# A two-block kernel on one core: which accumulator pair a stream begins on, and where its residuals stand

## What is computed

```python
hx = _rmsnorm(x, norm_g[l]) * (1.0 + scale) + shift        # scale, shift, gate: silu(c) @ w_mod[l]
hc = _rmsnorm(ctx, norm_g[l]) * (1.0 + scale_c) + shift_c
q, k, v, g_att, u_pool, g_pool, a_conv, b_conv, g_conv = split(hx @ w_in[l])
...
y = concat([y_att * silu(g_att), y_pool * silu(g_pool), y_conv * silu(g_conv)])
x = x + gate * (y @ w_out)                                  # and for ctx in layer 0
```

## Time and profile before

| | us |
|---|---|
| median of 3 runs (2693.75 to 2694.1) | 2694.1 |
| the profiled execution | 2695.04 |
| its span | 2693.1 |
| TensorE busy in it | 2604.9 (97%) |
| VectorE busy | 1701.3 (63%) |
| ScalarE busy | 1259.4 (47%) |
| mean granted TensorE clock | 0.993 of full |

### The profile page before, as it was taken

The page is one execution under the profiler, slowest core; times in us unless marked ns, Lnnn a source line. Parts: engine busy times, 40 slices in busy tenths (PEclk is TensorE's granted clock), DMA queues, the critical chain, the costliest instruction groups (busy, mean ns, idle before and its releaser), DMA issues.

```text
span 2693.1 us, 34021 instructions
## 1 busy us (share of the span) xinstructions
PE 2604.9 (97%) x12453; PEld 2064.8 (77%) x12453; DVE 1701.3 (63%) x2483; ACT 1259.4 (47%) x1734; POOL 101.0 (4%) x147
## 2 busy tenths in 40 slices
PE   7999999999999999798999999999999999999997
PEld 5888888888877776565788787678878886788876
DVE  5565755656644444354678856388985664688855
ACT  4544544545533333343356553345554443345553
POOL 0000000000000000000200000020000000200000
PEclk9999999999999999899999999999999999999999
DMA  7555555555568888868854567864446758844454
GB/s 239 172 183 169 179 174 172 165 180 172 171 235 289 291 275 293 279 242 324 277 168 157 168 239 261 314 213 139 161 150 219 244 185 317 279 141 156 136 182 152
DMA packets 350381, 569.62 MB, mean 212 GB/s; under 512 B 18096, under 2 KB 202832, under 8 KB 346272
## 3 DMA queue, kind: packets, MB, share of 16 engines
q1 hardware_dynamic: 343248, 531.48, 58.0%
q0 software_dynamic: 6992, 36.18, 3.9%
HBM read 559.17 MB, written 8.42 MB: 211 GB/s over the span
## 4 chain that ended last, share of the span: by engine, by line
PE 81%; DVE 8%; issue 4%; DMA 4%; ACT 2%; SPq 1%; DVEq 1%; POOL 0%; ACTq 0%
PE acc L451 24%; PE acc L453 23%; PE acc L452 23%; PE aux L971 3%; DMA raw<-in_w_mod 2%; DVE w_lo L439 2%; PE aux L1173 1%; DVE cacc L2332 1%; DVE sm L2264 1%; PE aux L1306 1%; ACT w_hi L431 1%; PE aux L1146 1%; DMA xr_s<-x_mid 1%; DMA xr_s<-c_mid 1%; PE aux L878 1%
## 5 line engine op out<-in xcount | busy, mean ns | idle before, releaser
L439 DVE TENSOR_TENSOR w_lo<-raw,w_hi 128x1024 fp32r<-128x1024 f32 x808 | 989.1, 1229 | 763.6 <-ACT w_hi L431 761.8
L431 ACT ACTIVATE w_hi<-raw 128x1024 fp32r<-128x1024 f32 x808 | 846.7, 1058 | 928.4 <-PE acc L453 867.3
L451 PE MATMUL acc<-w_hi,h_hi 128*128 128x512 f32 x2240 | 894.7, 399 | 11.6 <-DVE w_lo L439 4.5
L453 PE MATMUL acc<-w_hi,h_lo 128*128 128x512 f32 x2240 | 873.6, 390 | 0.0
L452 PE MATMUL acc<-w_lo,h_hi 128*128 128x512 f32 x2240 | 873.4, 390 | 0.0
L451 PEld LDWEIGHTS acc<-w_hi,h_hi 128*128 128x128 f32 x2240 | 421.0, 188 | 145.0 <-issue 53.1
L453 PEld LDWEIGHTS acc<-w_hi,h_lo 128*128 128x128 f32 x2240 | 420.7, 188 | 90.3
L452 PEld LDWEIGHTS acc<-w_lo,h_hi 128*128 128x128 f32 x2240 | 421.4, 188 | 81.9
L451 PE MATMUL acc<-w_hi,u_hi 128*128 128x512 f32 x800 | 320.7, 401 | 4.4 <-ACT cT L1765 2.3
L452 PE MATMUL acc<-w_lo,u_hi 128*128 128x512 f32 x800 | 312.1, 390 | 0.0
L453 PE MATMUL acc<-w_hi,u_lo 128*128 128x512 f32 x800 | 312.0, 390 | 0.0
(11 more groups left out here) (348 smaller groups left out, 1892.1 us busy)
## 6 DMA issues: line engine op xcount, KB each, us to landing
raw<-in_w_in SPq DMA_DIRECT2D x632, 512.0 KB, 4.4
raw<-in_w_mod SPq DMA_DIRECT2D x192, 512.0 KB, 6.1
raw<-in_w_out SPq DMA_DIRECT2D x96, 512.0 KB, 5.0
raw<-in_w_rnn_out SPq DMA_DIRECT2D x32, 512.0 KB, 5.1
raw<-in_w_o SPq DMA_DIRECT2D x32, 512.0 KB, 6.1
raw<-in_w_attn_out SPq DMA_DIRECT2D x16, 512.0 KB, 5.8
xr_s<-x_mid POOLq DMA_DIRECT2D x4, 1024.0 KB, 12.6
xo<-x_mid POOLq DMA_DIRECT2D x4, 1024.0 KB, 8.0
```

The lines of the kernel that those rows point to most:

```text
L431: act.activation(w_hi[:, n % NSPLIT], raw[:, slot, (n % 2) * SK:(n % 2) * SK + SK], ACT.Copy).then_inc(hi_ready, 1)
L439: dve.tensor_tensor(w_lo[:, n % NSPLIT], raw[:, slot, (n % 2) * SK:(n % 2) * SK + SK], w_hi[:, n % NSPLIT].bitcast(F32), ALU.subtract).the ...
L451: pe.matmul(acc[pair][m][:, :], a_hi[:, k0 + k, tok], w_hi[:, s, k], start=b, stop=False)
L453: last = pe.matmul(acc[pair][m][:, :], a_lo[:, k0 + k, tok], w_hi[:, s, k], start=False, stop=e)
```

## The change

Two things, both in the hand-written order. First, `FLIP` gives each stream a bit; stream x0 has 1. All its accumulator uses are turned over, on each engine: the first four parts, the head parts, the transposes that borrow a pair, the last input part and the output parts. `pair_free` for x0 and c1 now waits for residual 2's reads in part 0 and for residual 3's in part 1. Second, residuals 0 to 2 of each tail stand at `out_end(c) + 4` (25, 27 and 35), and residual 3 at granule 4 of the following stream. PE's waits for parts 2 and 3 stay as they were.

```diff
+        FLIP = (0, 1, 0, 0)
...
-                    pe.wait_ge(*ST[s - 1].at("res", 2 * NT * (NCH - 1) + NT) if c == 0 else ST[s - 1].at("res", 2 * NT * (NCH - 1)))
+                    pe.wait_ge(*ST[s - 1].at("res", 2 * NT * (NCH - 2 + c) + NT))
...
-                        products(pe, q, n, c % 2, 2 * g, a_hi, a_lo, g == 0, g == 7)
+                        products(pe, q, n, (c + flip) % 2, 2 * g, a_hi, a_lo, g == 0, g == 7)
...
-                    products(pe, q, n, (c + 1) % 2, 2 * j, b_hi, b_lo, j == 0, j == 7)
+                    products(pe, q, n, (c + 1 + flip) % 2, 2 * j, b_hi, b_lo, j == 0, j == 7)
...
+                pair = [acc[(i + FLIP[s]) % 2] for i in range(2)]
...
-                    if n == 1:
+                    if n == 4:
                         last_stage_end()
...
-                    if s == 1 and n == 1:
+                    if s == 1 and n == 4:
                         last_stage_end()
...
-                        dve.tensor_tensor(ytmp[:, m], acc[(c + 1) % 2][m][:, :], gbc[:, cs], ALU.mult).then_inc(S["res"], 1)
+                        dve.tensor_tensor(ytmp[:, m], pair[(c + 1) % 2][m][:, :], gbc[:, cs], ALU.mult).then_inc(S["res"], 1)
...
                     for c in range(NCH - 1):
-                        if n == out_end(c) + 2:
+                        if n == out_end(c) + 4:
                             residual(c)
```

More of the change, by code:

```diff
@@ L1278, in stream @@
                             for j in range(4):
-                                last = pe.transpose(acc[1][m][:, j * P:(j + 1) * P], cacc[:, j, m * P:(m + 1) * P], ident[:, :])
+                                last = pe.transpose(acc[1 - flip][m][:, j * P:(j + 1) * P], cacc[:, j, m * P:(m + 1) * P], ident[:, :])
                         last.then_inc(S["cb_ps"], 1)
@@ L1288, in stream @@
                             for m in range(NT):
-                                last = pe.transpose(acc[1][j // 2][:, (2 * (j % 2) + m) * P:(2 * (j % 2) + m + 1) * P],
+                                last = pe.transpose(acc[1 - flip][j // 2][:, (2 * (j % 2) + m) * P:(2 * (j % 2) + m + 1) * P],
                                                     tcy[:, m, j * P:(j + 1) * P], ident[:, :])
@@ L1690, in stream @@
                         done(3)
-                        act.activation(stg[:, 1], acc[0][1][:, :], ACT.Copy).then_inc(S["ev_act"], 1)
+                        act.activation(stg[:, 1], pair[0][1][:, :], ACT.Copy).then_inc(S["ev_act"], 1)
                     if n == 31:
@@ L1703, in iteration @@
                                 done(4)
[L1704 to L1705 removed]
+                                act.activation(stg2[:, 0], pair[1][0][:, :], ACT.Sigmoid)
+                                act.activation(stg2[:, 1], pair[1][1][:, :], ACT.Sigmoid).then_inc(S["ev_act"], 1)
                             if n == 8:
@@ L1731, in iteration @@
                             act.wait_ge(*S.at("qkT_ps", 2 * p))
-                            act.activation(qk2[:, 1], acc[0][1][:, :], ACT.Copy).then_inc(S["ev_act"], 1)
+                            act.activation(qk2[:, 1], pair[0][1][:, :], ACT.Copy).then_inc(S["ev_act"], 1)
                         if n == 15:
@@ L2362, in stream @@
                             dve.wait_ge(*ST[2].at("kT_ps", 2))
-                        dve.tensor_copy(stg[:, 0], acc[0][0][:, :]).then_inc(S["ev_dve"], 1)
+                        dve.tensor_copy(stg[:, 0], pair[0][0][:, :]).then_inc(S["ev_dve"], 1)
                     if n == 19:
@@ L2427, in iteration @@
                             dve.wait_ge(*S.at("qkT_ps", 2 * p))
-                            dve.tensor_copy(qk2[:, 0], acc[0][0][:, :]).then_inc(S["ev_dve"], 1)
+                            dve.tensor_copy(qk2[:, 0], pair[0][0][:, :]).then_inc(S["ev_dve"], 1)
                             if not rotary:
@@ L2449, in conv_norm @@
                         for m in range(NT):
-                            step.link(dve.bn_stats(bns[:, m], acc[1][m][:, :]))
+                            step.link(dve.bn_stats(bns[:, m], pair[1][m][:, :]))
                         step.wait(dve)
@@ L2460, in conv_norm @@
                         for m in range(NT):
-                            step.link(dve.tensor_scalar(tcy[:, m], acc[1][m][:, :], sm[:, 48 + 2 * m:49 + 2 * m], sm[:, 46 + m:47 + m],
+                            step.link(dve.tensor_scalar(tcy[:, m], pair[1][m][:, :], sm[:, 48 + 2 * m:49 + 2 * m], sm[:, 46 + m:47 + m],
                                                         ALU.subtract, ALU.mult))
```

33 lines of the change are left out of this document (17 added, 16 removed).

## The result

The changed kernel is slower: 2705.3 us (median of 7 runs, 2703.2 to 2708.5) against 2694.3 for the kernel before (7 runs, 2693.8 to 2700.5), a ratio of 1.0032 with a 95% interval of [1.0022, 1.0041]. A second measurement gave 2704.3 against 2696.7, 1.0028 [1.0018, 1.0039]. The forecast was 2701.0, in a range of 2694.5 to 2705.5.

What follows compares the result with a forecast made beforehand. TensorE, busy 97% of the span, was taken as the bound, so only its pauses count. Tails +5.9, clock +4.2, stream starts -3.4, `w_mod` granule +0.9, x1's tail -0.7: +6.9 us, median 2701.0, range 2694.5 to 2705.5.

Steps and rivals of the forecast that it cites:

- Part 1, the tails: Tails of c0 and x0: residual 0 behind the sums delays TensorE before granule 24; net +2.95 and +2.93, together +5.9 us.
- Part 2, the clock: Behind each new 3.9 us tail pause the clock likely falls to half, 8 in 10 each; +4.2 us for both.
- rival A: Tail pauses come but the clock holds in both or one: 2696.8 us, or 2698.9 with one fall; chance 0.22.
- Part 3, the stream starts: Starts of x0 and c1: TensorE's wait for residual 3 to free `acc[0]` goes at both; -3.4 us.
- Part 3, the third `w_mod` granule: Start of x0: the later `c_mid` write meets this granule's load; +0.9 us, bounds -1 to +3.
- Rival C: Start of x0: `c_mid` write costs its upper bound and the fourth `w_mod` granule is late too; 2704 us, chance 0.11.
- Part 4: Tail of x1, without normalization: `lo(24)` and `lo(25)` run first and residual 0 frees the pair in time; -0.7 us.
- Rival B: Early tails: the `xr_s` load lands early enough that residual 0 is not held; -5.4 us, 2688.7, chance 0.11.
- Rival D: Stream starts gain nothing, as a late split granule or last normalization replaces the wait; +3.4 us, 2704.4, chance 0.06.

Runs made afterwards that it cites:

- second profile: Profile of the changed kernel, unedited, measured once more beside the kernel before: 2704.3 us, ratio 1.0028 [1.0018, 1.0039].

## Why the prediction was right, and where its sizes were off

**Part 1, the tails.** Right. TensorE was due at 1606.76 and 2084.54 (the last matmul before the pause, plus 0.227 us) and went on at 1610.89 and 2088.75: 4.13 and 4.21 us late, against 4.08 and 4.03 forecast. The pauses before 26 are gone, and so is that of the last tail; residuals 1 and 2 cost nothing.

**Part 2, the clock.** Right in kind and a little too dear: a fall behind each pause, 1.7 us each in the first profile against 2.1 forecast. In the second profile TensorE resumed at 1606.58 with the clock already at half, and it was back at 1612.8: 6.2 us of work at half, 3.1 lost, by this stretch:

```profile
1612.00:1613.00 1.00, 1.00 (x5) 0.76 (x4) 0.97 (x3) 0.84 (x1) 0.00 (x0) 0.60 0.92 256
```

The net of each tail, pause and clock, is +4.6 and +4.8 by the time from the stage's first matmul to the normalization's transposes (51.37 and 51.46 us, against 46.73 and 46.71); forecast +5.0 each. The chances did not fit each other: 8 in 10 for each fall leaves 0.36 for rival A if the two are independent, not 0.22.

**Part 3, the stream starts.** The waits went as said. The step at each start is 0.23 us where it was 1.81, so -1.6; what S3 leaves after its tail is -1.9; forecast -1.7 each. c1's ScalarE waits 1.91 us for its rows, forecast 2, and no one waits for it.

**Part 3, the third `w_mod` granule, is the term that was mis-sized**: +0.9 taken, bounds -1 to +3. It waits 3.31 instead of 1.01 us, and the clock fell behind it, 1.7 us more: about +4. In the second profile no fall, but 3.51 + 0.80 us of waits: +3.3.

Two things were off. The first is the landing. Counted from the last matmul of c0 (1650.61 before, 1659.81 after), TensorE asked for the granule at 19.10 instead of 20.78, so 1.7 us earlier, just as forecast. It got it at 22.41 instead of 21.79, so 0.6 later, where +0.9 means about 0.8 earlier. The issue by SyncE, forecast 0.6 earlier, came at 10.91 instead of 10.95, and its two transfers took 2.79 us to go out instead of the 1.06 of the earlier trace rows:

```profile
1670.72 2.79 SPq L377 DMA_DIRECT2D raw<-in_w_mod  x2
```

The second is the clock, which the forecast priced in the tails only. Rival C named the place and took the upper bound; its number, 2704, is nearer.

**Part 4.** -1.1 against -0.7.

The sum over the touched stages by these measures is 4.6 + 4.8 - 1.6 - 1.9 + 3.8 - 1.1 = +8.6 (the table's +8.7, rounded otherwise), against +6.9 forecast; the 3.8 is what S1 leaves after its tail and start. With +4.6 ahead of S1, -1.0 in S2 and 0 in S4, from the clock's falls there, this is the +12.1 between the two profiled spans. The medians differ by 11.1 in the first measurement and by 7.6 in the second. Most runs behind them have no profile, so how much of that the falls make up is not shown.

That the first time lay within the range is in part luck. It is above the forecast's own range (2698.5 to 2703.5) and 0.2 us below the upper end of the whole. The forecast also stood on 2694.1 for the kernel before, of which later medians were 2696.7 to 2696.9.

Rival A did not occur: the clock fell behind both tail pauses in both profiles of the change. Rival B was decided by the landing of the rows, as it said, and the run with the load first shows it from the other side. Rival D did not occur: the step at both starts is 0.23 us.

## What to carry to other kernels

In an order written out by hand, an instruction that frees a buffer for TensorE must stand ahead of anything on its engine that waits for a transfer, and one place in the list can be worth 5 us. Count a pause of TensorE of 3 us or more with what the clock may take behind it; here two waits of 1.4 to 1.7 us were cheaper than one of 3.3 to 3.5 with a fall. When a wait is removed shortly ahead of a stretch that is fed by transfers, look there for the gain before you book it. And before explaining a difference of a few us between two profiles, compare the stages that no edit touched, and the clock in them.

## What the hardware showed that was not expected

- Behind these pauses the clock was at half for one of two lengths. After 3.97 and 4.05 us of pause that was about 3.4 us; after 4.41 us it was 6.8, and took 3.1 us of work instead of 1.7. The length of the pause does not decide which: 3.45 us brought 3.4 us at half in one kernel, and 6.8 in the one with residual 0 at granule 24. Its stretches, TensorE resuming at 1671.29:

```profile
1670.00:1671.00 1.00, 0.00 (x0) 0.00 (x0) 1.00 (x2) 0.00 (x0) 0.00 (x0) 0.62 1.04 410
1671.00:1672.00 1.00, 0.71 (x4) 0.11 (x8) 0.16 (x1) 0.00 (x0) 0.00 (x0) 0.50 1.03 340
...
1676.00:1677.00 1.00, 1.00 (x4) 0.81 (x3) 0.00 (x0) 0.00 (x0) 0.00 (x0) 0.50 0.99 391
1677.00:1678.00 1.00, 1.00 (x5) 0.77 (x5) 0.00 (x0) 0.00 (x0) 0.00 (x0) 0.97 1.04 393
```

- Nor does a length decide whether it falls, near 3 us: two pauses of 2.94 us (residual ahead of the sums) brought falls, one of 3.51 did not. The two pauses of the earlier trace rows, 2.96 and 2.93 us, stand in all 14 profiles within 0.01 us: a fall came with the first in 9 of them and with the second in 10. So the forecast's pair, one on each side, said nothing about the place. All pauses of 3.9 us and more that were looked at brought a fall; those of 1.4 to 1.7 us in x0's head did not.
- Stages that no edit touched differ by up to 6 us between profiles of nearly equal kernels (1568.7 to 1574.9 us ahead of S1). The two longest, 1573.9 and 1574.9, are also those with the most time at half clock there, two more falls of 3.4 and 6.8 us than in the kernel before. A change worth 2 us does not show in one span; it shows in a stage's length once the falls of the clock in that stage are counted.
